# Issuing the expert rows' transfers from SP's queue instead of ACT's, and the next layer's parameters earlier

## The reference

```python
def _hier_moe(h, p):                        # h: 384 tokens x 1024
    gl = h @ p['w_group_router']            # 4 groups, the best one is taken
    el = h @ p['w_expert_router']           # 4 experts in a group, the best two
    ...
    for gi in range(N_GROUPS):
        a = jnp.einsum('bsd,edf->bsef', h, p['w_e1'][gi])
        b = jnp.einsum('bsd,edf->bsef', h, p['w_e3'][gi])
        y = y + jnp.einsum('bsef,efd->bsd', jax.nn.silu(a) * b * w_all[:, :, gi, :, None], p['w_e2'][gi])
```

## Time and profile before

| | us |
|---|---|
| median of 3 runs | 2133.7 (2126.93 to 2134.96) |
| the profiled execution's own time | 2134.96 |
| its span, first to last instruction | 2133.2 |
| PE busy | 2028.3 (95%) |
| DVE busy | 745.5 (35%) |
| ACT busy | 470.3 (22%) |
| POOL busy | 69.8 (3%) |

### The profile page before, as it was taken

One profiled execution on the slowest core, in us unless ns is written; L12 is line 12 of the kernel. 1 busy time (PEld: TensorE's weight loads), 2 busy tenths in 40 slices (PEclk: granted clock), 3 DMA queues, 4 the chain that ended last, 5 costly groups with the idle time before them and its releaser, 6 DMA issues.

```text
span 2133.2 us, 29796 instructions
## 1 busy us (share of the span) xinstructions
PE 2028.3 (95%) x12706; PEld 1102.4 (52%) x12706; DVE 745.5 (35%) x1981; ACT 470.3 (22%) x926; POOL 69.8 (3%) x97
## 2 busy tenths in 40 slices
PE   6999999999999979999989999999999997999997
PEld 3454556556555544444345565665655555444433
DVE  1281676323311131222244677532341113122224
ACT  2211234344200121111023122334430012111111
POOL 0000100000000010000010010000000001000001
PEclk9999999999999989999999999999999998999998
DMA  9676561221122448999932213112313244899992
GB/s 387 254 266 260 194 240 44 87 92 72 64 114 99 197 153 329 390 394 394 397 141 79 98 68 121 45 49 82 119 60 118 79 182 165 301 391 393 391 401 100
DMA packets 43576, 416.60 MB, mean 195 GB/s; under 512 B 5424, under 2 KB 5552, under 8 KB 17328
## 3 DMA queue, kind: packets, MB, share of 16 engines
q1 hardware_dynamic: 30240, 369.53, 44.5%
q10 hardware_dynamic: 6720, 23.60, 3.1%
q0 software_dynamic: 6480, 21.51, 2.8%
HBM read 386.03 MB, written 28.58 MB: 194 GB/s over the span
## 4 chain that ended last, share of the span: by engine, by line
PE 84%; DMA 10%; DVE 3%; issue 1%; ACT 1%; POOL 0%; SPq 0%; POOLq 0%; DVEq 0%; ACTq 0%
PE psum L733 16%; PE psum L1016 16%; PE psum L1117 8%; PE psum L1031 8%; PE psum L736 6%; PE psum L1138 5%; DMA pc<-we_in 5%; PE psum L1122 4%; PE psum L1059 4%; DMA ring<-we_in 2%; PE psum L654 2%; PE psum L847 2%; DMA ring<-wch_in 1%; DMA ring<-wmod_in 1%; PE psum L711 1%
## 5 line engine op out<-in xcount | busy, mean ns | idle before, releaser
L733 PE MATMUL psum<-hT,ring 128*128 128x384 f32 x1088 | 369.3, 493 | 2.0 <-ACT pc L1310 1.9
L1016 PE MATMUL psum<-hT,ring 128*128 128x384 f32 x1024 | 346.6, 492 | 0.0
L733 PEld LDWEIGHTS psum<-hT,ring 128*128 128x128 f32 x1088 | 203.1, 192 | 144.1 <-issue 19.0
L1016 PEld LDWEIGHTS psum<-hT,ring 128*128 128x128 f32 x1024 | 193.8, 191 | 133.0 <-issue 3.3
L1031 PE MATMUL psum<-pc,ring 128*128 128x384 f32 x512 | 175.6, 486 | 0.0
L1745 DVE SCALAR_TENSOR_TENSOR pc<-pc,par 128x128 f32<-128x128 f32 x480 | 159.5, 417 | 0.0
L2182 DVE TENSOR_TENSOR ytok<-pc,psum 128x384 f32<-128x384 f32 x32 | 17.7, 554 | 345.7 <-ACT pc L1583 345.7
L2135 DVE COPY scr<-psum 64x512 f32<-64x512 f32 (+1 forms) x180 | 91.8, 510 | 123.7 <-PE psum L1138 122.1
L1031 PEld LDWEIGHTS psum<-pc,ring 128*128 128x128 f32 x512 | 95.4, 190 | 62.9 <-issue 1.5
L1117 PE MATMUL psum<-ring,scr 128*64 128x512 f32 x512 | 116.9, 609 | 10.6 <-issue 10.3
L736 PE MATMUL psum<-ring,hT 128*128 128x512 f32 x288 | 126.1, 594 | 0.0
(11 more groups left out here) (341 smaller groups left out, 2097.0 us busy)
## 6 DMA issues: line engine op xcount, KB each, us to landing
ring<-we_in SPq DMA_DIRECT2D x48, 2048.0 KB, 19.0
pc<-we_in SPq DMA_DIRECT2D x48, 2048.0 KB, 18.8
ring<-wmod_in SPq DMA_DIRECT2D x42, 1024.0 KB, 6.1
ring<-wch_in SPq DMA_DIRECT2D x18, 2048.0 KB, 8.7
ring<-wgate_in SPq DMA_DIRECT2D x16, 2048.0 KB, 7.8
ring<-wbr_in SPq DMA_DIRECT2D x16, 1024.0 KB, 7.6
ring<-wtok_in SPq DMA_DIRECT2D x6, 2048.0 KB, 7.8
expert_out_rows<-scr ACTq DMA_DIRECT2D x30, 384.0 KB, 9.5
```

The costliest lines, as they stand in the source:

```text
L733: mm = pe.matmul(F[:, 0:T], wv[:, k, n * P:(n + 1) * P], hT[:, k, :], start=k == 0, stop=k == KD - 1)
L1016: mm = pe.matmul(bank(5 + n % 2)[:, 0:T], wv[:, k, (n % 4) * P:(n % 4 + 1) * P], hT[:, k, :], start=k == 0, stop=k == KD - 1)
```

## The change

The two helper functions move from ACT's program to SP's, with their waits, and so do all their calls. In each turn e of SP's loop, which now runs over all 16 experts, the order is: wait for `hidden(e)`, fill slots 0 and 1 of expert e + 2; wait for `turn_rows(e + 1)`, `load_rows(e + 3)`; in turn 3 of layer 0 `load_early(1)` and `load_params(1)`; wait for `project(e - 1)`, fill slot 2 of expert e + 1; `store_rows(e - 1)`. In turn 14 the store comes ahead of the fill. The waits on the last stores that ACT and POOL have stay as they were.

```diff
-                for e in range(NE - 1):
+                def load_rows(e):
+                    sp.dma_start(x_rows[e % 2], xs_d[e * CAP:(e + 1) * CAP, :]).then_inc(rows_in[e % 2].sem, 16)
+
+                def store_rows(e):
+                    sp.wait_ge(xy_ready.sem, xy_ready.at(l, 2 * e + 2))
+                    sp.dma_start(ys_d[e * CAP:(e + 1) * CAP, :], x_y[e % 2]).then_inc(y_stored[e % 2].sem, 16)
+
+                sp.wait_ge(scattered.sem, scattered.at(l, scattered.per_layer))
+                load_rows(1)
+                load_rows(2)
+                for e in range(NE):
                     if e < NE - 2:
                         sp.wait_ge(xab_done.sem, xab_done.at(l, e + 1))
                         fill(l, ("exp", e + 2, 0))
                         fill(l, ("exp", e + 2, 1))
-                    if e >= 1:
+                    if e < NE - 3:
+                        sp.wait_ge(xt_done.sem, xt_done.at(l, e + 2))
+                        load_rows(e + 3)
+                    if l + 1 < DEPTH and e == 3:
+                        load_early(l + 1)
+                        load_params(l + 1)
+                    if e == NE - 2:
+                        store_rows(e - 1)
+                    if 1 <= e < NE - 1:
                         sp.wait_ge(xy_done.sem, xy_done.at(l, 2 * e))
                         fill(l, ("exp", e + 1, 2))
-                if l + 1 < DEPTH:
-                    load_early(l + 1)
-                    load_params(l + 1)
+                    if e >= 1 and e != NE - 2:
+                        store_rows(e - 1)
...
-                ac.wait_ge(scattered.sem, scattered.at(l, scattered.per_layer))
-                load_rows(1)
-                load_rows(2)
                 for e in range(NE):
-                    if e == NE - 1:
-                        store_rows(e - 1)
                     ac.wait_ge(xab_done.sem, xab_done.at(l, e + 1))
...
                     if e + 1 < NE:
                         copy_rows(e + 1)
-                    if e < NE - 3:
-                        load_rows(e + 3)
                     ac.wait_ge(xgt_done.sem, xgt_done.at(l, e + 1))
                     ac.activation(mva_flat[:, 0:4 * CAP], bank(4)[:, 0:4 * CAP], ACT.Copy).then_inc(xgt_ready.sem, 1)
-                    if 1 <= e < NE - 1:
-                        store_rows(e - 1)
```

## The result

| | us |
|---|---|
| before, median of 4 runs | 2130.3 (2124.13 to 2134.96) |
| after, median of 4 runs | 2151.6 (2145.82 to 2158.08) |
| after / before | 1.0108, 95% interval 1.0082 to 1.0135 |

The changed kernel is 1.1% slower; the forecast was 0.4% less, with 2138 as the upper end of its range. A repeat of six runs gave 1.0103 (1.0086 to 1.0121). A ratio is taken over all the runs and not from the two medians, and the two ways differ by up to 0.1%. The rows here are of the repeat's profiled execution, since outside the experts' stages it resembles that of before; the last experiment says why that matters.

The account below looks back on a forecast made before the run. In the expert stages DMA was taken to be slightly slower than PE, 18.0 us an expert against 17.34. Terms -0.1 - 0.6 - 5.4 - 1.8 = -7.9 us gave 2126 us against the median of 2133.7, range 2118 to 2138.

Parts of the forecast that it names:

- Row loads in the fills' queue: Experts 3 to 15, each layer: a load beside weights gets 0.35 us cheaper in SP's queue, -4.6 us a layer.
- Rival C: Fills of slots 0 and 1: row loads and stores as blocks hold weights up, +12.2 us, 2145.9; chance 0.06.
- Rival A: Expert stages: one queue changes nothing for row loads, each still costs 2.4 us; +3.0 us, 2136.7; chance 0.29.
- Stores behind the fills: End of each expert stage: expert 12's store no longer overtakes the deciding fill, -0.9 us in each layer.
- rival B: Expert stages: row loads become as cheap as alone, PE is the bound again; -14.7 us, 2119.0; chance 0.25.
- Early weights and parameters: Turn 3, layer 0: 2.31 MB now ahead of expert 14's slot 2, +5.4 us on the deciding landing.
- The last store of layer 0: End of layer 0's expert stage: without the parameters beside it, the last store lands 0.6 us sooner.
- ACT's relief: Expert stages: ACT loses 30 row loads, 30 stores and two kinds of waits while PE waits for DMA; worth 0.
- SP's order: SP's loop: the added waits delay no needed fill, and rows and stores still come in time; worth 0.
- The clock behind the wait: `project(14)`, each layer: without the wait ahead of it, it runs at full speed, 1.8 us less.
- The sum: Landing for `project(14)`: -0.1 us in layer 0, -5.5 in layer 1; whole kernel -7.9 us, 2126 us against 2133.7.

Follow-up runs that it names:

- the last experiment: The kernel before, unchanged, profiled again on the third chip as a control: span 2144.2 us, expert stages 248.9 and 248.2 us.
- the fastest kernel: The kernel before with only the stores moved to SP's queue, row loads staying on ACT's: 2127.8 us against 2142.8, ratio 0.9939.

## Why the prediction was wrong

**"Row loads in the fills' queue" is the step that failed**, by its sign. It put the worth of a load between 0 and 1.1 us saved, took a third of that as -4.6 us a layer, and bounded the loss at 0.35 us each. With nothing else moved, the loads in the fills' queue cost 10 us of the kernel's time, 7.1 us of layer 0's stage and 0.5 of layer 1's. Together with the stores they lose by the dips about 0.5 us each, 13 x 0.5 = 6.5 us a layer, and with all that belongs to it 7.08 MB at 380 GB/s for 395 in layer 0 and 375 for 392 in layer 1, so 0.7 and 0.8 us an expert, 9 to 11 us over 13. Rival C had the sign and the place, but its chance of 0.06 and its price (2145.9) were too small. The argument against it, that sums of bytes stay the same and the blocks are small, is one about bytes, and bytes were not what a load cost. The argument that the engines' being out of step leaves a third of the gain has no support either: with the blocks in the queue the tail ahead of the deciding landing is some 3 us longer than before, so the spread of the engines was not a fixed background in which blocks are placed. But it isn't shown to be the cause of the loss, since kernels that lose nothing have such tails.

**Rival A's premise fell too.** It held that the second queue isn't the cause, with stores as its proof. By the rule of the Trainium skill in "DMA: Bandwidth & Descriptors", section "Issuing engines are not separate DMA queues", which A rested on, the issuer would matter only for issue time. Here it made +0.5% for the loads, -0.6% for the stores and +0.9% for both, with nothing else moved. At 128 partitions the rule holds as far as these runs can tell: 0.9959 and 0.9945 for one queue and two, with overlapping intervals, and fills that land after 14.9 and 15.4 us.

**"Stores behind the fills" failed too.** It counted only the one overtaking store, -0.9 us a layer, whatever queue the loads are in. In the changed kernel's order, with the loads on SP already, the stores there cost 7 us more (2147.5 for 2140.3), most of it in layer 1's stage (256.4 for 249.3). With the loads left on ACT they gain 13 to 15 us: 5.0 and 5.3 us in the stages, which is all that PE can take, and 1.7 us for each `project(14)`. That is about rival B's gain (14.7 us, from PE as the bound again), but from an edit that I had costed at next to nothing; that B's number comes out there says nothing for B's reason.

**"Early weights and parameters"**: +5.4 us forecast for the landing, +6.4 in the profile of that part alone; in the median the part makes +2.8 (interval 1.1 to 6.8) against a forecast of 5.4 - 0.6 = 4.8. Right within the interval.

**The last store of layer 0**: 2.96 us to landing for 3.60, -0.6 as forecast. **ACT's relief and SP's order at 0**: right as far as the rows go; the chain has SP's issue 0.01 us behind its event, and PE never waits for rows or ACT's copies in this stretch. **The clock behind the wait**: `project(14)` takes 5.52 us once the wait is gone, 7.2 with it (and 7.9 at a granted clock of 0.51 in the window ahead of it in the changed kernel, which is near the lower level of 1.2 GHz; what came before is 4.2 us without work). The -1.8 us was right in mechanism, but in the changed kernel the wait it hung on grew, and one earlier wait in each layer cost another 1.7 us in the same way (8.78 and 8.79 us for 7.09).

**The sum.** For the landing ahead of `project(14)` I had -0.1 and -5.5 us; measured +12.3 and +11.1. With +6.4 us for the parameters (as alone), layer 0 leaves 5.9 us for the queue, and layer 1 all of its 11.1; alone, the queue's part gave 9.0 and 7.6. The two differ by 3 us a layer, and two profiles of the changed kernel by 2, so a finer split than that can't be had from one profile each.

**Open.** Why a load to 96 partitions costs more as a block within the fills' queue than as single packets from another one, why moving the stores away makes the loads cheaper, why stores help with the loads on ACT and harm with them on SP (+10 to +17 us), and why the loads alone hurt layer 0 and hardly layer 1. That the loss goes with 96 partitions is shown; that the engines' drifting apart is its mechanism is not: the tails are 4.7 us before, 7 to 8 in the changed kernel, 7 with 128-row loads in the same order, and some 4 us in the fastest kernel. Nothing here measured single engines against ports, and a kernel with loads to 64 partitions, or with the rows of a load split over two, wasn't tried.

## What to carry to other kernels

When a small transfer lowers the rate of large ones beside it by more than its bytes explain, look at its number of partitions before its queue: 128 in place of 96, even with a third more bytes, was worth 0.5% here with two queues and 1.3% with one, and left no loss from the one queue that could be seen. "The same 16 engines serve all queues" fixes the bytes and not the rate at which they move, 375 to 409 GB/s here by the queues and the order of issues alone; so a blind change of queue deserves a real chance of loss when the stream is the bound. And try the parts of a change alone: the stores that I took for harmless lowered or raised the loss by the queue that the loads were in, and moved alone they were as good as any edit here.

## What the runs showed of the hardware that was not expected

- A 384 KB load from DRAM to 96 partitions costs a full weight stream 2.3 us in another queue than the fills' (0.93 for its bytes), 2.5 in the same queue, 2.8 there with the stores in it too, and 1.5 in another queue from which the stores are gone. These are estimates from the dips in two or three windows each; by a whole stage's mean the last is 1.6 to 1.9.
- The engines' mean share falls through 0.73, 0.40 and 0.15 in 6 us while a 2 MB fill is outstanding with nothing behind it (0.55 and 0.25 in 4 us in the fastest kernel): such a fill's last part lands at a low rate, whatever the queues.
- A store of the same 384 KB, from 96 partitions, has no such cost beside the weights (422 GB/s), but moving it to another queue changed the cost of the loads.
- Two profiled executions of the same kernel had spans 11 us apart with the expert stages equal within 0.6 us, so profiles are compared stage by stage.
